# Turning conditioning rows on TensorE: one full-width matmul for each 128 columns, or four in column groups

## What is computed

```
def adaln(c, w, b):
    m = (jax.nn.silu(c) @ w + b)[:, None, :]
    return jnp.split(m, 3, axis=-1)

def modulate(x, g, shift, scale):
    return rms_norm(x, g) * (1 + scale) + shift
...
shift, scale, gate = adaln(c_prompt, attn_ada_w[ia], attn_ada_b[ia])
h = modulate(xp, attn_norm_g[ia], shift, scale)
...
xp = xp + gate * (o @ attn_w_out[ia])
```

## Time and profile before

| | |
|---|---|
| median of 3 runs | 1191.11 us (1190.86 to 1195.8) |
| span of the profiled execution | 1178.2 us; the page gives no other time of it, and the median lies 12.9 us above |
| TensorE busy with matmuls, with weight loads | 86%, 64% of the span |
| VectorE, ScalarE, GpSimd busy | 36%, 21%, 12% |
| DMA | 215.12 MB, mean 183 GB/s |

### The profile page before, as it was taken

How to read it: one execution, slowest core, us unless ns; L and a number is a source line. 1 busy time by engine, 2 the same in 40 slices (tenths; PEclk the granted TensorE clock), 3 DMA queues, 4 the chain that set the end, 5 groups by cost and what they waited for, 6 DMA issues and landing times.

```text
span 1178.2 us, 21097 instructions
## 1 busy us (share of the span) xinstructions
PE 1019.0 (86%) x8404; PEld 751.0 (64%) x8404; DVE 423.6 (36%) x901; ACT 248.7 (21%) x538; POOL 137.7 (12%) x180
## 2 busy tenths in 40 slices
PE   4867999945886869989999999974789799999998
PEld 2646533432234655667888888854668588878886
DVE  0434039887132635424993200048711300000000
ACT  3344121112033424312133320040110211100001
POOL 2000000101023210000111111111121011111110
PEclk9779989986896758998999999987799899999999
DMA  9984449999884492308544443354264344443440
GB/s 322 347 284 118 180 153 319 361 330 356 343 283 136 139 352 71 88 15 234 173 143 144 143 143 120 131 179 146 79 196 133 108 136 149 143 142 131 155 142 37
DMA packets 105580, 215.12 MB, mean 183 GB/s; under 512 B 20560, under 2 KB 53136, under 8 KB 105401
## 3 DMA queue, kind: packets, MB, share of 16 engines
q0 software_dynamic: 40160, 153.20, 38.4%
q1 hardware_dynamic: 63434, 57.81, 15.5%
q10 hardware_dynamic: 1904, 2.94, 0.7%
HBM read 210.63 MB, written 7.48 MB: 185 GB/s over the span
## 4 chain that ended last, share of the span: by engine, by line
PE 72%; DMA 9%; DVE 8%; issue 5%; ACT 3%; SPq 2%; DVEq 0%; POOL 0%; ACTq 0%; POOLq 0%
PE psum L1219 20%; PE psum L1228 20%; DMA sb_arena<-in_cache_moba_kv 6%; PE psum L1444 5%; PE psum L643 4%; PE psum L791 3%; PE psum L1203 2%; PE psum L827 2%; DVE sb_sq L2000 2%; DVE sb_sq L2004 2%; PE psum L702 2%; DMA sb_ring<-in_attn_ada_w 1%; PE psum L715 1%; DMA sb_arena<-in_cache_nsa_kv 1%; PE psum L924 1%
## 5 line engine op out<-in xcount | busy, mean ns | idle before, releaser
L1219 PE MATMUL psum<-sb_hT,sb_ring 128*128 128x264 f32 x1024 | 232.6, 390 | 13.3 <-ACT sb_hT L1493 6.8
L1228 PE MATMUL psum<-sb_arena,sb_ring 128*128 128x264 f32 x1024 | 230.8, 388 | 2.6 <-DVE sb_arena L2247 2.4
L1219 PEld LDWEIGHTS psum<-sb_hT,sb_ring 128*128 128x128 f32 x1024 | 196.6, 193 | 47.5 <-issue 6.8
L1228 PEld LDWEIGHTS psum<-sb_arena,sb_ring 128*128 128x128 f32 x1024 | 195.4, 191 | 36.9 <-issue 3.2
L643 PE MATMUL psum<-sb_cst,sb_arena 128*128 128x128 f32 (+4 forms) x457 | 78.6, 310 | 36.0 <-DMA sb_arena<-in_cache_nsa_kv 9.0
L643 PEld LDWEIGHTS psum<-sb_cst,sb_arena 128*128 128x128 f32 (+4 forms) x457 | 56.0, 156 | 55.0 <-issue 22.6
L2254 DVE SCALAR_TENSOR_TENSOR sb_xT<-psum,sb_mods,sb_xT 128x256 f32<-128x256 f32 (+1 forms) x16 | 7.7, 484 | 224.9 <-PE psum L1228 224.9
L827 PE MATMUL psum<-sb_ring,sb_hT 128*128 128x512 f32 (+1 forms) x192 | 79.4, 566 | 0.0
L2247 DVE TENSOR_TENSOR sb_arena<-sb_arena x16 | 19.7, 1256 | 126.5 <-ACT sb_arena L1728 107.6
L827 PEld LDWEIGHTS psum<-sb_ring,sb_hT 128*128 128x128 f32 x192 | 35.5, 190 | 44.2 <-issue 39.9
L579 POOL DMA_DIRECT2D sb_ring<-in_mlp_w x28 | 24.8, 885 | 310.7 <-issue 147.9
(11 more groups left out here) (422 smaller groups left out, 1110.2 us busy)
## 6 DMA issues: line engine op xcount, KB each, us to landing
sb_ring<-in_mlp_w POOLq DMA_DIRECT2D x64, 1024.0 KB, 6.0
sb_arena<-in_cache_moba_kv SPq DMA_DIRECT2D x108, 256.0 KB, 7.1
sb_ring<-in_attn_ada_w POOLq DMA_DIRECT2D x6, 2048.0 KB, 22.2
sb_ring<-in_mlp_ada_w POOLq DMA_DIRECT2D x6, 2048.0 KB, 11.5
sb_ring<-in_ssm_ada_w POOLq DMA_DIRECT2D x6, 2048.0 KB, 17.6
sb_ring<-in_mlp_ada_w POOLq DMA_DIRECT2D x12, 1024.0 KB, 6.8
sb_ring<-in_attn_w_in POOLq DMA_DIRECT2D x5, 2048.0 KB, 11.3
sb_arena<-in_cache_nsa_kv SPq DMA_DIRECT2D x64, 128.0 KB, 2.9
```

Source lines behind the costliest of these rows:

```text
L1219: last = mm(bank[m % 4][:, 0:T], panels[:, j, 256 * k + P * ch:256 * k + P * ch + P], hT[:, k, :], start=(k == 0), stop=(k == KC - 1))
L1228: last = mm(bank[2 * pair + c][:, 0:T], panels[:, j, 256 * f + P * c:256 * f + P * c + P], actT[:, 8 * j + f, :], start=(j == 0 and f == 0 ...
```

## The change

Each block of 128 features is turned by one matmul with 128 weight columns instead of four with 32. The sums are the same, and the PSUM columns written are the same. A turn has 4 matmuls instead of 16; waits, semaphores, the order of the work and all other engines stay as they are.

```diff
@@ turn_back
                     for ch in range(4):
-                        for g in range(4):
-                            c = P * (ch % 2) + 32 * g
-                            last = mm(dst[32 * g:32 * g + 32, (4 * i + ch) * 9:(4 * i + ch) * 9 + 9], row(i)[:, ch // 2, c:c + 32],
-                                      cst[:, C_SL:C_SL + 9], start=True, stop=True)
+                        last = mm(dst[:, (4 * i + ch) * 9:(4 * i + ch) * 9 + 9], row(i)[:, ch // 2, P * (ch % 2):P * (ch % 2) + P],
+                                  cst[:, C_SL:C_SL + 9], start=True, stop=True)
                     last.then_inc(N.ada_tr, 1)
@@ late_turn
                 for ch in range(4):
-                    for g in range(4):
-                        c = 256 + (4 * j + ch) * 9
-                        last = mm(bank[7][32 * g:32 * g + 32, c:c + 9], late_rows[j][:, P * ch + 32 * g:P * ch + 32 * g + 32],
-                                  cst[:, C_SL:C_SL + 9], start=True, stop=True)
+                    c = 256 + (4 * j + ch) * 9
+                    last = mm(bank[7][:, c:c + 9], late_rows[j][:, P * ch:P * ch + P], cst[:, C_SL:C_SL + 9], start=True, stop=True)
                 last.then_inc(N.ada_tr, 1)
```

## The result

| | before | after |
|---|---|---|
| median, 20 executions each on one chip | 1187.8 us (1179.23 to 1198.11) | 1192.57 us (1183.92 to 1205.41) |
| ratio | | 1.0059 [1.0036, 1.0081], so +7.0 us, 4.3 to 9.6 |
| ratio of a second comparison (35 and 12 executions) | | 1.0047 [1.0016, 1.0077], +5.6 us |
| span of the profiled execution | 1178.2 us | 1185.8 us |
| its mean granted clock | 0.909 | 0.905 |

The account below looks back on a forecast made before the run. TensorE's dense stretches were taken to bound the kernel (72% of the chain). Terms 2.0 + 0.7 + 3.1 + 4.1 + 1.65 = 11.5 us gave 1202.6 us, 1.0% slower, range 1194.5 to 1209.

Parts of the forecast that it names:

- the wait of 11.65 us: TensorE's wait for VectorE's scores, ending at 266.27 us: forecast to shrink from 15.52 us by some 4 us.
- late turns 3 to 5: Turns among full-array work at 880.34 us: 24 passes taking 2.7 us instead of 1.05, +1.65 us.
- late turns 0 to 2: Three turns in a row at 842.44 us (L1339), read as half clock: 5.4 us instead of 1.37, +4.1; lower end +2.0.
- the base: Starting time for the sum: profiled span 1178.2 us plus an unchanged 12.9 to the runs' median, 1191.11 us.
- first projection, turns 0 to 4: L692: first three on the path, 2.6 us taken as +2.0; next two, 1.3 us, hidden in a 4.51 us DMA wait.
- first projection, turn 5: Half-clock turn at 74.21 us that VectorE's L1823 waits for: L1823 moves from 75.22 to 75.9, +0.7 us.
- second projection: Six turns beside the input projection: 4.6 us more on TensorE, covered by its 15.52 us wait for VectorE, cost 0.
- third projection: Six turns: the first hidden before a wait for cache values, five in busy 307 to 324 us; +3.1 us, nothing absorbing it.
- absorbed: Rival: transfers set stage ends up to 354 us, so only late turns cost, 3.65 to 5.75 us; chance 0.16.
- The falling clock: Rival: long rows of turns drop TensorE to half clock at 307 to 324 or around 880 us, +4 to +8; chance 0.15.
- Equal columns: Rival: pass cost follows weight columns alone, so turns add only ways in and out, 1191 to 1194 us; chance 0.02.
- The code rival: Rival: TensorE's code arrival sets the pace near 842 us, so three turns there cost nothing; 1195 to 1198.5 us; chance 0.08.

Follow-up runs that it names:

- second comparison: The unedited change run again against the kernel before, in the batch of the held-back panel kernels: ratio 1.0047 [1.0016, 1.0077].
- the kernel with the first projection alone: Only the first projection's six turns made full-width, all else as the kernel before: ratio 0.9994 [0.9968, 1.0020].
- the second kernel with the panels held back and column groups: Repeat of: POOL issues the six input-projection panels only after the cache's last page is turned, against the kernel before; ratio 0.9936 [0.9906, 0.9967].
- 72 full-width passes: The three late turns ahead of L1330 made full-width and each done three times, against the kernel before: ratio 1.0094 [1.0059, 1.0128].
- the 288 passes: The three late turns ahead of L1330 kept in column groups but each done three times, against the kernel before: ratio 1.0067 [1.0035, 1.0099].

## Why the prediction was wrong

The mechanism at the turns was right: four column groups load and multiply side by side, full-width loads follow each other 0.11 us apart, and the kernel is slower by it. What failed is what the prediction carried on from there: it took the first and the third projection's turns for work on TensorE's path, and both stand ahead of waits for transfers that took up some 4 and 0.9 to 2.5 us. Of the signs it named, the passes' spacing, the first turn of 1.0 us, the wait of 11.65 us and the late turns 3 to 5 (2.59) came as said; the stretch from 307 to 324 took 18.6 us instead of about 20, and late turns 0 to 2 took 2.78 instead of 5.4. The rule under which 16 loads of 32 columns equal 4 of 128 (the Trainium skill, "TensorE: Matmul & The Clock Gate", LDWEIGHTS) does not hold across column groups: 0.28 us for 32 passes stands against 0.9 for 8. Another section of that page of the Trainium skill, on the array as 16 blocks of 32 by 32, says that one block may multiply while others load. The trace agrees and goes further: the narrow loads also overlap each other, 28 of 0.11 us each within 0.36. The size was wrong in these terms and in the base:

| step | forecast | at the turns | what was left |
|---|---|---|---|
| first projection, turns 0 to 4 | +2.0 | +2.5 to +3.8 | about -0.6 behind the pages' wait |
| first projection, turn 5 | +0.7 | +1.1 | +0.55 |
| second projection | 0 | +3.2 by 250 us | 0 |
| third projection | +3.1 | +3.5 | +1.6 (+1.6 to +2.4 in four kernels) |
| late turns 0 to 2 | +4.1 | +1.4 to +4.0 | +0.2 to +3.3, not settled |
| late turns 3 to 5 | +1.65 | +1.56 | +1.56 |
| sum | +11.5 | | +3.3 to +6.4 |

The timed +7.0 (4.3 to 9.6) and +5.6 us (1.9 to 9.1) agree with the last column within their intervals.

*First projection.* "I take 2.0 ... All this is carried on" failed. The cost at the turns is read from the first turn to the instruction at 64.06, at equal clock: 39.4 us in the change and 36.5 to 37.1 in three kernels with column groups, each with 10.2 us at half clock, so +2.5; and 41.0 in the kernel with the first projection alone against 37.4 before, both with 13.7 us at half clock, so +3.6 (the second kernel with the panels held back and column groups needs 39.8 there, which stays unexplained). With 17.1 us at half clock two kernels with full-width turns need 42.6 and 42.7 and five with column groups 38.7 to 38.9, so +3.8. The working had 2.6 for turns 0 to 2 and 1.3 for 3 and 4, and that price was right. Then the wait of 64 to 73 us, in which turns 3 and 4 alone were said to vanish, took up 3.95. From the first turn to the end of that wait the three kernels with full-width turns and the panels in flight need +0.5, -0.9 and -1.3 us against column groups at equal clock. In the terms of the prediction this is the rival "absorbed", right for this place: the pages were late because the DMA engines were full, and TensorE coming later did not make them later by as much. The 11.53 us of DMA on the chain read 8.21 after. The sentence "TensorE gates these loads by freeing buffers", used against it, is true of the buffers and did not decide.

*Third projection.* "I see nothing to absorb it" failed. The value matmuls of 312.09 were taken for busy time; they held some 2 us of waiting for the cache's values, which the page shows as no idle time, and 0.9 to 2.5 us of the turns went into it in four kernels. A window that is "busy 16.34 of 17" was not full.

*Late turns 0 to 2.* The price at half clock was right (5.22 and 15.46 us for 24 and 72 passes). The working took one execution's clock and one execution's stops for the rule. The two profiles of the change have these turns at full clock, 2.78 us, the lower bound of the working, and mostly at half, 4.41 us; the column groups, at 1.37 us, had one of their better executions, as seven in eleven ran into a stop for code. In the mean the turns take 2.7 us in eleven kernels with column groups and 4.2 in five at full width. That the term of 4.1 was too large is likely and not shown.

*The base.* 12.9 us "above the span" do not exist. The profiled execution was one of the fastest, some 1180 us, and the three times shown were among the slower ones. On the true base of 1187.8 the sum of 11.5 would have given 1199.3, so the base accounts for 3.3 us of the miss of 10.0 and the sum for the rest.

*The other rivals.* The falling clock was not the cause: the change does not lower the mean granted clock. The trace of after has one fall at 107 to 117 us that the trace of before lacks, and others it lacks in turn. Equal columns is refuted by the passes' starts. The code rival, that late turns 0 to 2 cost nothing, is only just excluded by 1.0028 [1.0002, 1.0054] for them alone; against it speaks more that with 72 full-width passes 13.6 of 14.1 us stayed. Its mechanism, stops for code, is shown and takes part of their price.

## What to carry to other kernels

A matmul with few moving columns is paid by its weight load, and loads in separate column groups overlap: with 32 passes in 0.28 us against 8 in 0.9, quarter-width matmuls in four groups were the better form although they are four times as many instructions. Before a longer stretch is added to the sum, look for the next wait behind it and ask what that wait is for: one for a transfer on crowded queues took up the whole of the addition as far as these traces tell, and the gain lay in the crowd (holding six panels back gave 5.4 and 7.6 us). Long rows of pipelined matmuls may hold waits; compare their length with that of a full row of the same form.

## What the runs showed that was not expected

- The same program's profiled spans were 1178.2 and 1192.4 us, with mean granted clocks of 0.909 and 0.897. Where the clock falls differs from execution to execution; three times and one profile did not give the base to better than 0.3%. The clock records begin only at 21.29 us in the first trace and at 29.09 in the second, and the views print 1.00 ahead of that. The rows there have their half-clock length (16 passes in 3.64 us at 16.73, and 1.92 at 24.89 in the first trace), so a 1.00 ahead of the first record tells nothing.
- TensorE stops for 1.8 us between blocks of 128 passes, 256 instructions, when instructions are very short, though it waits for nothing that the profile shows as a wait; in column groups the 288 passes lost 3.62 us in this way and 72 full-width passes lost none. In the traces of four kernels a packet of code lands 1.2 to 1.6 us before such a stop ends.
- Panels that POOL had asked for at 58.89 and 64.18 us were asked for at 71.76 when they were held back. That cost next to nothing behind 81 us (from there to 249 us TensorE needed 0.3 us less than before in one trace and 0.6 more in the other) and made the kernel faster.
